# Latent attention: high and low parts of probabilities and values, and a value product in three rounded matmuls

## The reference, cut to what matters

```python
def block(args):                     # 128 queries at a time
    qn, qp = args
    sc = (jnp.einsum('bqhd,bkhd->bhqk', qn, k_nope, preferred_element_type=f32)
          + jnp.einsum('bqhr,bkr->bhqk', qp, k_pe, preferred_element_type=f32)) * scale
    p = jax.nn.softmax(sc, axis=-1)
    return jnp.einsum('bhqk,bkhd->bqhd', p.astype(v.dtype), v)
o = o.reshape(b, s, MLA_WIDTH) * jax.nn.silu(z)
```

## Time and profile before

| | before |
|---|---|
| median of 3 runs | 3251.09 us |
| profiled execution | 3247.69 us |
| its span, first to last instruction | 3245.9 us |
| latent attention, from its first projections to its last gate | about 1129 to 1636 us |
| TensorE busy (matmul) | 2845.2 us, 88% of the span |
| VectorE busy | 1728.6 us, 53% |
| ScalarE busy | 1330.6 us, 41% |
| granted TensorE clock, mean | 0.934 of full speed |

### The profile page before, as it was taken

How to read it: one execution, slowest core, us unless ns; L and a number is a source line. 1 busy time by engine, 2 the same in 40 slices (tenths; PEclk the granted TensorE clock), 3 DMA queues, 4 the chain that set the end, 5 groups by cost and what they waited for, 6 DMA issues and landing times.

```text
span 3245.9 us, 35611 instructions
## 1 busy us (share of the span) xinstructions
PE 2845.2 (88%) x13081; PEld 2245.6 (69%) x13081; DVE 1728.6 (53%) x2386; ACT 1330.6 (41%) x1897; POOL 0.2 (0%) x4
## 2 busy tenths in 40 slices
PE   2489999998789988899985899977698999999996
PEld 2368888887577766676764667644476878878785
DVE  5568888888544055555545445543455434434344
ACT  2256666665323133333323345644423513223232
POOL 0000000000000000000000000000000000000000
PEclk6699999999899999999997899988698999999998
DMA  5311111110211111212112210000021111111111
GB/s 179 126 50 46 46 45 45 45 39 25 71 46 36 54 53 45 67 48 69 58 52 90 56 33 20 27 7 7 1 98 38 42 53 46 41 50 44 53 36 68
DMA packets 217872, 166.97 MB, mean 51 GB/s; under 512 B 9563, under 2 KB 211251, under 8 KB 217779
## 3 DMA queue, kind: packets, MB, share of 16 engines
q1 hardware_dynamic: 217778, 165.74, 16.6%
HBM read 153.14 MB, written 12.58 MB: 51 GB/s over the span
## 4 chain that ended last, share of the span: by engine, by line
PE 76%; DVE 10%; ACT 6%; DVEq 3%; issue 2%; DMA 2%; ACTq 0%; SPq 0%
PE PS L425 17%; PE PS L426 17%; PE PS L427 17%; PE PS L895 4%; PE PS L1550 3%; PE PS L871 2%; PE PS L872 2%; DVE rest L416 2%; PE PS L882 2%; PE PS L1505 1%; PE PS L1540 1%; PE PS L2036 1%; PE PS L2049 1%; DVEq L1692 1%; PE PS L2060 1%
## 5 line engine op out<-in xcount | busy, mean ns | idle before, releaser
L425 PE MATMUL PS<-h_high,w_high 128*128 128x512 f32 x2176 | 880.3, 405 | 76.6 <-DVE w_low L447 27.1
L426 PE MATMUL PS<-h_low,w_high 128*128 128x512 f32 x2176 | 864.2, 397 | 0.0
L427 PE MATMUL PS<-h_high,w_low 128*128 128x512 f32 x2176 | 862.7, 396 | 0.0
L425 PEld LDWEIGHTS PS<-h_high,w_high 128*128 128x128 f32 x2176 | 419.9, 193 | 178.7 <-issue 68.9
L427 PEld LDWEIGHTS PS<-h_high,w_low 128*128 128x128 f32 x2176 | 418.2, 192 | 90.6
L426 PEld LDWEIGHTS PS<-h_low,w_high 128*128 128x128 f32 x2176 | 419.9, 193 | 84.7 <-issue 0.5
L447 DVE TENSOR_TENSOR w_low<-raw_weights,w_high 128x1024 fp32r<-128x1024 f32 (+2 forms) x161 | 185.3, 1155 | 236.4 <-ACT w_high L442 235.6
L442 ACT ACTIVATE w_high<-raw_weights 128x1024 fp32r<-128x1024 f32 (+2 forms) x161 | 160.8, 1001 | 273.2 <-PE PS L427 231.9
L667 DVE SCALAR_TENSOR_TENSOR residual<-PS,rest,residual 128x512 f32 (+1 forms) x112 | 83.2, 750 | 242.5 <-PE PS L427 238.0
L2520 DVE SCALAR_TENSOR_TENSOR gated<-rest,gated 128x1024 f32<-128x1024 f32 x44 | 56.5, 1285 | 254.7 <-ACT gated L2489 254.7
L1627 ACT ACTIVATE activations<-PS,rest 128x1024 f32<-128x1024 f32 x64 | 71.4, 1116 | 234.5 <-DVE rest L1693 234.5
(11 more groups left out here) (279 smaller groups left out, 4242.3 us busy)
## 6 DMA issues: line engine op xcount, KB each, us to landing
raw_weights<-in_w_in SPq DMA_DIRECT2D x61, 512.0 KB, 4.1
activations<-in_w_ada SPq DMA_DIRECT2D x16, 1536.0 KB, 7.0
raw_weights<-in_w_up SPq DMA_DIRECT2D x44, 512.0 KB, 3.8
activations<-in_ada_w SPq DMA_DIRECT2D x8, 1536.0 KB, 6.9
raw_weights<-in_w_out SPq DMA_DIRECT2D x24, 512.0 KB, 4.0
rest<-in_ada_w SPq DMA_DIRECT2D x16, 576.0 KB, 4.9
x_kept<-residual SPq DMA_DIRECT2D x2, 4096.0 KB, 13.0
residual<-x_kept SPq DMA_DIRECT2D x2, 4096.0 KB, 14.5
```

Source lines behind the costliest of these rows:

```text
L425: e.matmul(out_, wh[:, k, :], xh[:, k, cols], start=first, stop=False)
L426: e.matmul(out_, wh[:, k, :], xl[:, k, cols], start=False, stop=False)
L427: return e.matmul(out_, wl[:, k, :], xh[:, k, cols], start=False, stop=last_k)
```

## The change

The buffers PT and V become PTH and VH of type fp32r, and two more, PTL and VL, are laid into the region of the weight buffers, which has room beside the latent weights. ScalarE's two copies (of the transposed probabilities and of the values) write the high parts. VectorE gets two new kinds of instruction: the low part of the probabilities, once per block, and the low part of the values, twice per head. The value product becomes 24 fp32r matmuls in place of 8 f32 ones (16 instructions).

```diff
-        PT = R(NT, 2 * P)
-        V = R(NT, P)
+        PTH, VH = rounded("latent_probs_high", R.at(2 * S), NT, 2 * P), rounded("latent_v_high", R.at(S), NT, P)
...
+        PTL, VL = rounded("latent_probs_low", X.at(2 * S), NT, 2 * P), rounded("latent_v_low", X.at(S), NT, P)
...
             if m == 0:
-                e.wait_ge(rlA, 2 * t.h + 2)
+                e.wait_ge(vlow, 2 * t.h + 2)
+            out_ = banks(7)[:, (m % 2) * 2 * P:(m % 2 + 1) * 2 * P]
             for k in range(NT):
-                last = e.matmul(banks(7)[:, (m % 2) * 2 * P:(m % 2 + 1) * 2 * P], V[:, k, :], PT[:, k, :],
-                                start=(k == 0), stop=(k == NT - 1))
+                e.matmul(out_, VH[:, k, :], PTH[:, k, :], start=(k == 0), stop=False)
+                e.matmul(out_, VH[:, k, :], PTL[:, k, :], start=False, stop=False)
+                last = e.matmul(out_, VL[:, k, :], PTH[:, k, :], start=False, stop=(k == NT - 1))
             if m % 2 == 1:
                 last.then_inc(pv, 1)
...
         def act_evac(e, t, q):
             e.wait_ge(tr, 8 * t.h + (q + 1))
-            e.activation(PT[:, :, (q % 2) * P:(q % 2 + 1) * P], banks(5, 2).rearrange("p (a b) -> p a b", a=NT),
-                         ACT.Copy).then_inc(te, 1)
+            e.activation(PTH[:, :, (q % 2) * P:(q % 2 + 1) * P], banks(5, 2).rearrange("p (a b) -> p a b", a=NT),
+                         ACT.Copy).then_inc(th, 1)
...
+            if name[0] == "V":
+                e.wait_ge(rlA, 2 * t.h + (x + 1))
+                e.tensor_tensor(VL[:, 4 * x:4 * x + 4, :], src.rearrange("p (a b) -> p a b", a=4),
+                                VH[:, 4 * x:4 * x + 4, :].bitcast(F32), ALU.subtract).then_inc(vlow, 1)
+                return
...
+        def dve_low(e, t, q):
+            e.wait_ge(th, 8 * t.h + (q + 1))
+            cols = slice((q % 2) * P, (q % 2 + 1) * P)
+            e.tensor_tensor(PTL[:, :, cols], banks(5, 2).rearrange("p (a b) -> p a b", a=NT), PTH[:, :, cols].bitcast(F32),
+                            ALU.subtract).then_inc(te, 1)
...
                 if wanted(t, BEFORE.get(q), more):
                     dve_set(e, t, BEFORE[q])
+                dve_low(e, t, q)
                 if q == 1 and more and not t.odd:
                     dve_rope(e, 1, 2 * t.half + 2)
```

More of the change, by code:

```diff
@@ L1420, in latent_attention @@
         sc, mx, ex, pr = sem("la_scores"), sem("la_max"), sem("la_exp"), sem("la_probs")
-        tr, te = sem("la_tr"), sem("la_tr_out")
+        tr, th, te, vlow = sem("la_tr"), sem("la_tr_high"), sem("la_tr_out"), sem("la_v_low")
         pv, gt = sem("la_pv"), sem("la_gated")
@@ L1479, in pe_set @@
             elif name == "V1":
-                e.wait_ge(rlA, 2 * t.h + 1)
+                e.wait_ge(vlow, 2 * t.h + 1)
             elif name == "R0" or (name == "Q0" and not t.odd):
-                e.wait_ge(rlA, 2 * t.h + 2)
+                e.wait_ge(vlow, 2 * t.h + 2)
             elif name == "Q1":
@@ L1606, in act_set @@
             if name[0] == "V":
-                e.activation(V[:, 4 * x:4 * x + 4, :], src.rearrange("p (a b) -> p a b", a=4), ACT.Copy).then_inc(rlA, 1)
+                e.activation(VH[:, 4 * x:4 * x + 4, :], src.rearrange("p (a b) -> p a b", a=4), ACT.Copy).then_inc(rlA, 1)
             elif name[0] == "R":
@@ L1664, in dve_set @@
         def dve_set(e, t, name, init=False):
-            if name[0] == "V":
-                return
-            n = t if init else t.next()
             x = int(name[1])
@@ L1670, in dve_set @@
             hs = slice(x * HALF, (x + 1) * HALF)
+            if name[0] == "V":
[3 more added lines that the diff above has]
+                return
+            n = t if init else t.next()
             i = set_index(t, name, init) - (0 if init else 2)
```

## The result

The changed kernel takes 3346.9 us (median of six, 3340.82 to 3351.08); the kernel before 3250.4 in the same session. The ratio is 1.0293 (95% interval 1.0279 to 1.0308). It is slower, as forecast, but by 96.5 us and not by 70: the time lies 2 us above the stated range.

What follows compares the result with a forecast made beforehand. It took the order of VectorE's and ScalarE's work, not VectorE's total, as decisive: strict turns raise short steps. Terms summed to 69.6 us on 3247.7, giving 3317.3, so a median of 3321 us; range 3300 to 3345.

Steps and rivals of the forecast that it cites:

- 7 to 0, seven: From a head's last block maximum to the next head's first: 7.01 us against 4.02, seven times, 20.9 us in all.
- 0 to 1, heads 1 to 6: From block 0's maximum to block 1's, no modulation products: 5.78 us against 3.82, 11.8 us in all.
- 3 to 4, even heads: From block 3's maximum to block 4's, two modulation products: 7.01 us against 3.68, 13.3 us in all.
- 1 to 2, heads 1 to 6: From block 1's maximum to block 2's, behind the previous head's last value product: about 9.1 us against 8.58, 3.0 in all.
- 2 to 3, heads 0 to 6: From block 2's maximum to block 3's: about 9.45 us against 9.32, odd heads a little more; 2.1 us in all.
- head 7: Last head, no projections for a next head, so steps fall to the floor: 51.8 us against 39.70, 12.1 more.
- from the last maximum to the last gate: End of the latent stage, 11.0 us before: two low parts join the chain, the product is shorter; +3.5 us.
- all other steps: Block-to-block steps 4 to 5, 5 to 6 and 6 to 7, and 3 to 4 in odd heads: forecast to stay unchanged.
- the floors: Least step between maxima as VectorE and ScalarE take strict turns: 5.78 us, 7.01 with two modulation products; shorter steps rise.
- Rival 1: Latent stage: VectorE's free time hides the new work, TensorE gains shorter products; 3239 us, 5% (weaker form 3285, 3%).
- rival 2: Value product: 256-column fp32r matmuls take 0.23 us each, 5.5 us a product against 3.0; +50 us, 3371; 7%.
- Rival 3: TensorE's clock in the latent stage: one more half-speed stretch per head, some 2.5 us lost each; +20 us, 3341; 13%.

Runs made afterwards that it cites:

- the fill: The changed kernel with matmuls of a constant ahead of TensorE's waits, in two versions: 3336.5 and 3321.8 us.
- five places: The changed kernel with matmuls of a constant ahead of TensorE's waits at five kinds of place: 3321.8 us, ratio 1.0224 to the kernel before.
- Three filled places: The changed kernel with matmuls of a constant ahead of TensorE's waits at three kinds of place: 3336.5 us, ratio 1.0262 to the kernel before.

## Why the prediction was wrong, by its own steps

The sum was 69.6 us, the profiled execution has 93.1 more (3340.8 against 3247.7). Term by term, from the maxima of both traces:

| term | forecast | measured |
|---|---|---|
| 7 to 0, seven | 20.9 | 21.1 |
| 0 to 1, heads 1 to 6 | 11.8 | 12.8 |
| 3 to 4, even heads | 13.3 | 13.7 |
| 1 to 2, heads 1 to 6 | 3.0 | 3.0 |
| 1 to 2, head 0 | 2.9 | 2.6 |
| 2 to 3, heads 0 to 6 | 2.1 | 7.5 |
| head 7 | 12.1 | 14.9 |
| from the last maximum to the last gate | 3.5 | 7.5 |
| all other steps | 0 | 14.2 |
| outside these | 0 | -4.2 |

"All other steps" are mainly 4 to 5 (+9.9 over seven heads), 6 to 7 (+6.3), 3 to 4 in odd heads (+1.7) and 5 to 6 (-3.7, where the shorter product is waited for). What lies outside is no effect of the change that could be told from chance: behind the last gate thirteen profiled executions with the same code there have 1605 to 1614 us, and this one has the least.

The mechanism of the floors was right and its sizes were too: the low part 1.225 us for 1.22, the floors 5.68 and 7.09 for 5.78 and 7.01, the product's matmuls 0.12 us apart for 0.125. The rule from the Trainium skill, "TensorE: Matmul & The Clock Gate", section "Back-to-back issue gap" (109 ns for 256 columns), is 11 ns short of that, as it was 14 short of the wide ones. Rival 1 (VectorE's free time hides it) is refuted by the floors, rival 2 (narrow matmuls at the wide one's time) by the 0.12 us.

The step that failed is the last term, "4 to 5 (7.23 against 5.78), 5 to 6 and 6 to 7 (7.6 and 8.3 against 10 to 11): nothing", and with it the 2.1 us for 2 to 3, whose odd heads took 6.8 alone. A step that is longer than its floor was taken to keep its length. It does so only at the old clock: 4 to 5 and 6 to 7 of head 4 grew by 2.6 and 1.7 us at 0.65 and 0.86, and had their old lengths again when the fill brought the clock to 1.00. Rival 3, the clock, was kept apart from the forecast as another case with 13%, at 20 us. It belongs to the forecast's own mechanism. If TensorE works 422 us in 552 in place of 440 in 482, its idle time is 130 us and not 42, and the kernel before already fell to 0.73 in one stretch of a pair of heads. The prediction's own sign for this rival, long steps raised at a granted clock below 0.9, was seen (0.89) beside all the signs for the forecast.

The filled kernels put the clock's price at 21 us at least (in the stage of the two traces; 22 to 25 for the whole), and with five places three steps of odd heads still lacked 1.6 us each. Roughly, as smaller terms cancel, 69.6, 21 and 5 make 96 us, against 97.3 by which the stage grew.

The end, too, was undersized, by 4 us: its granted clock was 0.63, the last value product ran at 1.2 GHz (starts 0.21 us apart), and the last low part waited 3.5 us for its copy.

```profile
1726.53 1.22 DVE L1714 TENSOR_TENSOR latent_probs_low<-PS,latent_probs_high 128x1024 fp32r<-128x1024 f32 x1 [3.50 <-ACT latent_probs_high L1634]
```

```profile
1728.40 0.41 PE L1553 MATMUL PS<-latent_probs_high,latent_v_low 128*128 128x256 f32 x1
1728.62 0.41 PE L1551 MATMUL PS<-latent_probs_high,latent_v_high 128*128 128x256 f32 x1
```

What stays open: why a half-speed stretch falls where it does. Three filled places took the one in step 2 to 3 out of heads 3 and 5, five brought it back, and no run was made to tell which idle stretch calls it.

## What to carry to other kernels

Ask of a new instruction not whether its engine has time but what it waits for and what stands behind it in that engine's list. A wait for the other engine's later item turns two overlapping chains into one; walk one turn of both lists and add up. And when a change makes TensorE wait more, price the clock in the same sum, not as a rival: look for the half-speed stretches that are there already and ask what more idle time does to the long steps. Two changes of order, with no work removed, were worth 124 us here, more than the change had cost; some 20 of them were to be had in the kernel before too.

## What the runs showed of the hardware that was not expected

Work without a use can pay through TensorE's clock: matmuls of a constant ahead of waits, 34 to 38 in a head, took 10 us off the changed kernel, and 66 to 70 took off 22 to 25 us. At 1.2 GHz a rounded matmul of 256 columns starts 0.21 us after the one before and one of 512 columns 0.43, at 2.4 GHz 0.12 and 0.23. A shorter value product alone gave back a quarter of what it saved (4.4 of 18 us). In its trace 6 to 7 in even heads and 3 to 4 in odd heads, at a lower clock (0.86 for the first in head 4), together took 9 us back; the rest was saved where TensorE was not waited for.
